# A hybrid decoder layer on one core: the bias row's table loaded by GpSimd, its product moved to the start, the fourth tile turned half a block earlier

## The chip, the cores and the metric

The kernel runs on one core of a Trainium2 chip. Its time is the device time of one execution in microseconds (us); 3 executions of the kernel before gave a median of 664.41 us (664.1 to 664.52). Five engines of the core work side by side, each on its own list of instructions, and wait for each other only through semaphores: TensorE (PE: matrix products, and transposes as products with an identity), ScalarE (ACT), VectorE (DVE), GpSimd (POOL) and SyncE (SP), which here only issues DMAs. GpSimd and ScalarE can issue DMAs too, each into a queue of its own. "Turning" a tile means transposing it on PE.

## The reference

One layer, cut to what matters here. The input is 512 rows of 1024 numbers.

```python
h = rmsnorm(x, norm_pre_mix)                 # (512, 1024)
proj = h @ w_in                              # f, q, i, g; aq, ak, av; indexer iq, ik, iw
y_a = hgrn2_mixer(...)                       # gated linear recurrence, 4 heads of 128
y_b = dsa_mixer(..., rel_bias)               # 128 keys of the indexer's choice per query, 8 heads of 64
    # bias = rel_bias[t5_bucket(qpos - key)] # rel_bias: (32 buckets, 8 heads), added to the logits
x = x + rmsnorm(concat(y_a, y_b) @ w_o, norm_post_mix)
h = rmsnorm(x, norm_pre_ffn)
x = x + rmsnorm((silu(h @ w_gate) * (h @ w_up)) @ w_down, norm_post_ffn)
```

The bias depends only on the distance between query and key. So it is enough to have, for each head, one row of 640 values by distance: the table (32 x 8) turned and multiplied with a one-hot matrix (32 x 640) that says which bucket each distance falls in.

## The kernel before, in words

All float32 numbers are split into a high part (rounded to the format of PE's faster passes) and a low part (the remainder); each large product is then three products: high x low, low x high, high x high. The high part is made on ScalarE by a copy, the low part on VectorE by a subtraction.

**The start.** The 512 rows are four tiles of 128 rows. Each tile t is loaded (`s_x[t]`), squared and summed on ScalarE (`square_in(t)`, L739 and L741), its inverse root is taken on GpSimd (`inv_of`, L617), VectorE scales it with root and gain (`scale_in(t)`, L1096, `s_hx`), PE turns it with eight transposes (`turn_in(t)`, L1670, `s_hps`), ScalarE copies the high part out of PSUM (`turn_hi`, L730, `s_hhi`) and VectorE takes the low part (`turn_lo`, L1089, `s_hlo`). The gain row is spread over the partitions by two products (L1770) ahead of that. Between them PE runs transposes of the identity into an unused bank as fillers (`keep_busy`, L1759).

The first weight chunk (256 columns, `iq`) is loaded and split in two halves of four blocks (`s_raw_half`, `s_raw[0]`; L1101, L631, L745, L1106). PE multiplies it first with the two tiles that are ready (`first_rows(half, m, w, x)`, L1779, 256 columns, four products a call) and later, once the low part of the fourth tile is there (`s_hlo` = 4), with the other two in `feature_group` (L1626). From then on each chunk is done in full by `project(g)` (L1626), 512 columns at a time. Weight chunks come in through a ring of two buffers that SyncE fills (L573), each when the low part of an earlier one is made.

**The bias row.** SyncE loads table and one-hot (L564, L565) behind the tiles and the first chunk, counted on `s_small` together with two other small loads (L562, L563). PE forms the row in two products (L1805, L1806: 8 x 512 and 8 x 128) into banks 6 and 7, ScalarE copies it to SBUF (L758, L759, `s_gsb`), stores it to memory (L763, `s_grow`), and GpSimd later spreads it from there (L652).

Nothing decides the order at run time: each engine's list is in the order in which its program is written, and each DMA queue takes its transfers in order of issue.

Of the kernel before, what the change touches and what calls it, by code (L numbers as in the profile page):

```python
# [7 lines left out]
P = 128  # L8
# [4 lines left out]
ACT = mybir.ActivationFunctionType  # L13

HEADS_A, DK = 4, 128
HEADS_B, DH = 8, 64
# [18 lines left out]
def hymba_layer(nc, x, w_in, lb_logits, hgrn_gnorm, rel_bias, w_o, norm_pre_mix, norm_post_mix,  # L35
                norm_pre_ffn, norm_post_ffn, w_gate, w_up, w_down, onehot, out):
    _, S, D = x.shape
# [69 lines left out]
    with ExitStack() as ctx:  # L107
        def sb(name, shape, dt=F32):
            return ctx.enter_context(nc.sbuf_tensor(name, shape, dt))

        def sem(name):
            return ctx.enter_context(nc.semaphore(name))

        PS = ctx.enter_context(nc.psum_tensor("PS", [P, 8, 512], F32))
# [3 lines left out]
        hT_hi = sb("hT_hi", [P, KT, S], F32R)  # L118
# [81 lines left out]
        oh_sb, tab, g_sb = A2[0:N_BUCKETS, 4096:4736], A2[0:N_BUCKETS, 4736:4744], A2[0:HEADS_B, 4768:5408]  # L200
# [21 lines left out]
        s_ones = sem("row_of_ones")  # L222
        s_gps0 = sem("gain_in_psum")
        s_small = sem("small_landed")
        s_raw = [sem(f"raw_landed{i}") for i in range(2)]
        s_ikw = sem("ikw_raw_landed")
        s_raw_half = sem("first_w_half_landed")
# [23 lines left out]
        s_gps = sem("bias_row_psum")  # L251
        s_gsb = sem("bias_row_sbuf")
# [156 lines left out]
        def ring_of(j):  # L409
            return j if j < J_IKW else j - 1  # L410

        def raw_view(j):
            if j == J_IKW:
                return raw_ikw.rearrange("p (k n) -> p k n", k=KT)
            return view(raw[:, ring_of(j) % 2, :], j)
# [26 lines left out]
        def ring3(n):  # L442
            return W_f[:, RING[n % 3], :]
# [6 lines left out]
        def step_raw(d):  # L450
            return W_f[:, WL[d % 4], :]
# [103 lines left out]
        @block.sync  # L555
        def _(sp):
            for t in range(TB):
                if t == 2:
                    sp.dma_start(raw_view(0)[:, 0:4, :], raw_src(0)[:, 0:4, :]).then_inc(s_raw_half, 16)
                sp.dma_start(xin[:, t, :], x_d[t * P:(t + 1) * P, :]).then_inc(s_x[t], 16)  # L560
            sp.dma_start(raw_view(0)[:, 4:8, :], raw_src(0)[:, 4:8, :]).then_inc(s_raw[0], 16)
            sp.dma_start(lbt[:, :, :], lb_logits.rearrange("r (h p) -> p r h", p=P)).then_inc(s_small, 16)  # L562
            sp.dma_start(gn[:, :], hgrn_gnorm.rearrange("a p -> p a")).then_inc(s_small, 16)  # L563
            sp.dma_start(tab, rel_bias).then_inc(s_small, 16)  # L564
            sp.dma_start(oh_sb, onehot).then_inc(s_small, 16)  # L565
            sp.dma_start(far[:, :], rel_bias[N_BUCKETS - 1, :].partition_broadcast(P)).then_inc(s_far, 16)
            for j in range(1, J_FF + 4):
                if j == J_IKW:
                    sp.dma_start(raw_view(j), raw_src(j)).then_inc(s_ikw, 16)
                    continue  # L570
                if ring_of(j) >= 2:
                    sp.wait_ge(s_lo, j - 2 if j - 2 <= J_IKW else j - 1)
                sp.dma_start(raw_view(j), raw_src(j)).then_inc(s_raw[ring_of(j) % 2], 16)  # L573
            for n, j in enumerate(range(J_FF + 4, J_DN)):
                if n < 2:
                    sp.wait_ge(s_lo, j - 1)
                elif n == 2:
                    sp.wait_ge(s_gu, 8)
                else:
                    sp.wait_ge(s_gu2, 2 * (n - 2))  # L580
                sp.dma_start(view(ring3(n), j), raw_src(j)).then_inc(s_raw3[n % 3], 16)
            for d, (kind, c) in enumerate(STEPS):
                if d == 0:
                    sp.wait_ge(s_gu2, 2 * (NS - 2))
                elif d < 3:
                    sp.wait_ge(s_prod, 3 * (NS - 2 + d))
                elif d == 3:
                    sp.wait_ge(s_gu2, 2 * NS)
                else:
                    steps_done(sp, d - 3)  # L590
                x, y = [wd[(2 * c + k) * P:(2 * c + k + 1) * P, :] for k in range(2)]
                if kind == "one":
                    sp.dma_start(step_raw(d)[:, 0:D], x).then_inc(s_dw[d % 4], 16)
                    sp.dma_start(step_raw(d)[:, D:D + 512], y[:, 512:D]).then_inc(s_dw[d % 4], 16)
                elif kind == "two":
                    sp.dma_start(step_raw(d)[:, 0:D], y).then_inc(s_dw[d % 4], 16)
                else:
                    sp.dma_start(view(step_raw(d), J_DN + c), raw_src(J_DN + c)).then_inc(s_dw[d % 4], 16)
            for t in range(TB):
                for half in range(2):  # L600
                    c = slice(half * 512, (half + 1) * 512)
                    sp.wait_ge(s_fin, 2 * t + half + 1)
                    sp.dma_start(out_d[t * P:(t + 1) * P, c], x2[:, t, c]).then_inc(s_out, 16)
            sp.wait_ge(s_out, 16 * 2 * TB)
# [3 lines left out]
        def _(pool):  # L608
            n_chain = [0]

            def link(ins):
                n_chain[0] += 1
                ins.then_inc(s_pool, 1)
                pool.wait_ge(s_pool, n_chain[0])
# [4 lines left out]
            def inv_root(col, n, width):  # L619
# [3 lines left out]
            link(pool.memset(ident[:, :], 0.0))  # L623
            pool.affine_select(out=ident[:, :], in_=ident[:, :], compare_op=ALU.not_equal, fill=1.0, base=0,
                               pattern=[[-1, P]], channel_multiplier=1).then_inc(s_const, 1)
            link(pool.memset(mhalf[:, :], -0.5))
            for t in range(2):
                pool.wait_ge(s_ss, norm("in", t))
# [93 lines left out]
        def _(act):  # L722
# [5 lines left out]
            def turn_hi(n, banks, t):  # L728
                act.wait_ge(s_hps, n + 1)
                act.activation(hT_hi[:, :, t * P:(t + 1) * P],  # L730
                               PS[:, banks:banks + 2, :].rearrange("p a (k t) -> p (a k) t", t=P),
                               ACT.Copy).then_inc(s_hhi, 1)

            act.dma_start(gain_row, norm_pre_mix).then_inc(s_gin, 16)
            def square_in(t):
                act.wait_ge(s_x[t], 16)
                if t:
                    act.wait_ge(s_sq, t)
                act.activation(ya[:, 0:D], xin[:, t, :], ACT.Square, accum_out=ss[:, t:t + 1]).then_inc(s_sq, 1)  # L739
                act.wait_ge(s_sq, t + 1)  # L740
                act.activation(ms[:, t:t + 1], ss[:, t:t + 1], ACT.Copy, scale=1.0 / D, bias=EPS).then_inc(s_ss, 1)  # L741
# [4 lines left out]

            square_in(0)
            square_in(1)
            turn_hi(0, TURN_BANK[0], 0)
            turn_hi(1, TURN_BANK[1], 1)  # L750
            square_in(2)
# [2 lines left out]
            turn_hi(2, TURN_BANK[2], 2)  # L754
            turn_hi(3, TURN_BANK[3], 3)
            split(1)
            act.wait_ge(s_gps, 1)
            act.activation(g_sb[:, 0:S], PS[0:HEADS_B, 6, :], ACT.Copy)  # L758
            act.activation(g_sb[:, S:S + P], PS[0:HEADS_B, 7, 0:P], ACT.Copy).then_inc(s_gsb, 1)  # L759
            act.wait_ge(s_lbm, 1)  # L760
            act.activation(lbw[:, 1:3, :], lbt[:, :, :], ACT.Exp).then_inc(s_lbe, 1)
            act.wait_ge(s_gsb, 1)
# [311 lines left out]
        def _(dve):  # L1074
# [46 lines left out]
            split_first_rest_lo()  # L1121
            turn_lo(2, TURN_BANK[2], 2)
            turn_lo(3, TURN_BANK[3], 3)
            dve.wait_ge(s_small, 64)
            link(dve.tensor_tensor(lbw[:, 0, :], lbt[:, 0, :], lbt[:, 1, :], ALU.max))
            for r in range(2):
                o = dve.tensor_tensor(lbt[:, r, :], lbt[:, r, :], lbw[:, 0, :], ALU.subtract)
# [495 lines left out]
        def _(pe):  # L1623
# [133 lines left out]
            def keep_busy(bank, n):  # L1757
                for _ in range(n):
                    pe.transpose(PS[:, bank, 0:P], ident[:, :], ident[:, :])  # L1759

            def turn_in(t):
                pe.wait_ge(s_hx, t + 1)
                turn(xin[:, t, :], TURN_BANK[t])
# [5 lines left out]
            for half in range(2):  # L1769
                o = pe.matmul(PS[:, 2 + half, :], pick_last, gain_in_last[:, half * 512:(half + 1) * 512], start=True, stop=True)  # L1770
            o.then_inc(s_gps0, 1)
            keep_busy(1, 9)
            turn_in(0)
            turn_in(1)
            keep_busy(1, 8)

            def first_rows(half, m, w, x):
                for k in range(4 * half, 4 * half + 4):
                    pe.matmul(PS[:, m, 0:S // 2], w[:, k, m * P:(m + 1) * P], x[:, k, 0:S // 2],  # L1779
                              start=(half == 0 and x is hT_hi and w is first_hi and k == 0),  # L1780
                              stop=(half == 1 and x is hT_lo and k == KT - 1))

            first_hi, first_lo = w_split(0)
# [9 lines left out]
                first_rows(0, m, first_hi, hT_lo)  # L1793
            turn_in(2)
            pe.wait_ge(s_hi, 1)
            for m in range(2):
                first_rows(1, m, first_hi, hT_hi)
            turn_in(3)
            pe.wait_ge(s_lo, 1)
            for m in range(2):  # L1800
                first_rows(1, m, first_lo, hT_hi)
            for m in range(2):
                first_rows(1, m, first_hi, hT_lo)
            pe.wait_ge(s_small, 64)
            pe.matmul(PS[0:HEADS_B, 6, :], tab, oh_sb[:, 0:S], start=True, stop=True)  # L1805
            pe.matmul(PS[0:HEADS_B, 7, 0:P], tab, oh_sb[:, S:S + P], start=True, stop=True).then_inc(s_gps, 1)  # L1806
            pe.wait_ge(s_hlo, TB)
            for m in range(2):
                feature_group(w_split(0), m, P, m, S // 2, S, s_proj)
# [291 lines left out]
```

## Time and profile before

| | us |
|---|---|
| median of 3 executions | 664.41 |
| the profiled execution | 664.47 |
| its span | 662.7 |
| PE busy | 652.5 (98% of the span) |
| VectorE busy | 535.2 (81%) |
| ScalarE busy | 343.6 (52%) |
| GpSimd busy | 91.8 (14%) |

The span is the time from the first to the last recorded instruction; 1.77 us of the execution lie around it. The profile is of one execution. In lists of instructions the first number is the start in us from the beginning of the span, the second the duration (several equal instructions that follow each other stand in one row, with xcount), and in brackets stands how long the engine was idle before and what released it. A float32 product is recorded as two pieces, so the two products of L1770 show as x4.

### The profile page before, as it was taken

The page shows a single profiled execution, that of the slowest core. Times are in us where ns is not written, and L with a number is a line of the kernel's source. Part 1 is how long each engine was busy: PE and PEld are TensorE (multiplying, and loading weights), DVE is VectorE, ACT ScalarE, POOL GpSimd, SP SyncE. Part 2 cuts the span into 40 slices and gives each one's busy share as a digit, 9 for nine tenths or more (in the row PEclk, how much of TensorE's full clock was granted, in tenths as well). Part 3 has the DMA queues.
Part 4 walks back from the last instruction along what each step waited for, and adds up shares of the span by engine and source line. Part 5 has one row for each costly group of instructions (what it writes and reads, how often), then busy time and mean ns, then how long its engine had stood idle before and what let it go on. Part 6 is the DMA issues. An engine that isn't in the chain of part 4 may idle for free.

```text
span 662.7 us, 10171 instructions
## 1 busy us (share of the span) xinstructions
PE 652.5 (98%) x4029; PEld 582.1 (88%) x4029; DVE 535.2 (81%) x746; ACT 343.6 (52%) x547; POOL 91.8 (14%) x131
## 2 busy tenths in 40 slices
PE   8999999999999999999999999999999999999996
PEld 6878888888888889888998999999999998888885
DVE  5766999998988768345986988989989879987845
ACT  5656433443349578234653555554555565644532
POOL 4800230000405378002100000000000000000000
PEclk9999999999999999999999999999999999999999
DMA  8443042343521300262342323334234235444513
GB/s 277 129 159 100 29 128 65 96 158 96 190 65 64 121 7 19 110 191 64 98 157 63 105 87 128 93 101 128 77 115 128 68 108 207 158 148 153 164 45 127
DMA packets 50946, 75.01 MB, mean 113 GB/s; under 512 B 5329, under 2 KB 40145, under 8 KB 50642
## 3 DMA queue, kind: packets, MB, share of 16 engines
q1 hardware_dynamic: 47040, 62.26, 29.6%
q0 software_dynamic: 3568, 11.55, 4.7%
q8 instruction: 32, 0.52, 0.3%
q10 hardware_dynamic: 290, 0.55, 0.2%
q14 instruction: 16, 0.13, 0.1%
HBM read 69.60 MB, written 6.84 MB: 115 GB/s over the span
## 4 chain that ended last, share of the span: by engine, by line
PE 94%; DVE 2%; ACT 1%; issue 1%; DMA 1%; POOL 0%; DVEq 0%; POOLq 0%; SPq 0%; ACTq 0%
PE PS L1626 38%; PE PS L1966 27%; PE PS L2004 12%; PE PS L2015 4%; PE PS L1845 2%; PE PS L1700 2%; PE PS L1676 1%; PE PS L1675 1%; PE PS L1856 1%; PE PS L1779 1%; PE PS L1670 1%; DMA A<-in_x_dram 1%; PE PS L1741 1%; PE PS L1710 1%; ACT A L905 1%
## 5 line engine op out<-in xcount | busy, mean ns | idle before, releaser
L1626 PE MATMUL PS<-hT_lo,w_hi 128*128 128x512 f32 (+2 forms) x280 | 102.0, 364 | 0.0
L1626 PE MATMUL PS<-hT_hi,w_hi 128*128 128x512 f32 (+2 forms) x280 | 100.7, 360 | 0.0
L1626 PE MATMUL PS<-hT_hi,w_lo 128*128 128x512 f32 (+2 forms) x280 | 100.7, 359 | 0.0
L1085 DVE TENSOR_TENSOR w_lo<-raw,w_hi 128x2048 fp32r<-128x2048 f32 x21 | 48.1, 2291 | 19.0 <-ACT w_hi L726 18.8
L1966 PE MATMUL PS<-hT_hi,W_r 128*128 128x256 f32 x216 | 61.1, 283 | 0.0
L1966 PE MATMUL PS<-hT_hi,s_w 128*128 128x256 f32 x216 | 61.1, 283 | 0.0
L1966 PE MATMUL PS<-hT_lo,s_w 128*128 128x256 f32 x216 | 61.1, 283 | 0.0
L1626 PEld LDWEIGHTS PS<-hT_hi,w_hi 128*128 128x128 f32 (+1 forms) x280 | 52.5, 188 | 8.4
L1626 PEld LDWEIGHTS PS<-hT_lo,w_hi 128*128 128x128 f32 (+1 forms) x280 | 52.6, 188 | 7.3 <-issue 0.2
L1626 PEld LDWEIGHTS PS<-hT_hi,w_lo 128*128 128x128 f32 (+1 forms) x280 | 52.6, 188 | 7.2
L1966 PE MATMUL PS<-s_t,s_w 128*128 128x256 f32 x288 | 57.8, 283 | 0.6 <-ACT PS L954 0.6
L1966 PEld LDWEIGHTS PS<-s_t,s_w 128*128 128x128 f32 x288 | 47.5, 192 | 0.8 <-issue 0.8
L726 ACT ACTIVATE w_hi<-raw 128x2048 fp32r<-128x2048 f32 x21 | 40.1, 1911 | 14.8 <-PE PS L1626 14.1
L1456 DVE TENSOR_TENSOR W_r<-W_f,s_w 128x1024 fp32r<-128x1024 f32 x36 | 44.0, 1223 | 1.2 <-ACT s_w L939 0.2
L1626 PE MATMUL PS<-w_lo,hT_hi 128*128 128x512 f32 x112 | 44.6, 398 | 0.0
L954 ACT ACTIVATE PS<-PS 128x256 f32<-128x256 f32 x54 | 19.9, 368 | 47.2 <-PE PS L1966 45.6
L1626 PE MATMUL PS<-w_hi,hT_hi 128*128 128x512 f32 x112 | 43.7, 390 | 0.0
L1626 PE MATMUL PS<-w_hi,hT_lo 128*128 128x512 f32 x112 | 43.6, 390 | 0.0
L1966 PEld LDWEIGHTS PS<-hT_lo,s_w 128*128 128x128 f32 x216 | 41.5, 192 | 0.0
L1966 PEld LDWEIGHTS PS<-hT_hi,W_r 128*128 128x128 f32 x216 | 41.5, 192 | 0.0
L1966 PEld LDWEIGHTS PS<-hT_hi,s_w 128*128 128x128 f32 x216 | 41.5, 192 | 0.0
L1966 PE MATMUL PS<-s_t,W_r 128*128 128x256 f32 x144 | 40.7, 283 | 0.0
(306 smaller groups left out, 1685.9 us busy)
## 6 DMA issues: line engine op xcount, KB each, us to landing
raw<-in_w_in_dram SPq DMA_DIRECT2D x15, 1024.0 KB, 5.5
W_f<-in_w_gate_dram SPq DMA_DIRECT2D x9, 1024.0 KB, 5.3
W_f<-in_w_up_dram SPq DMA_DIRECT2D x9, 1024.0 KB, 5.3
W_f<-in_w_down_dram SPq DMA_DIRECT2D x16, 512.0 KB, 3.5
raw<-in_w_o_dram SPq DMA_DIRECT2D x4, 1024.0 KB, 4.9
W_f<-in_w_down_dram SPq DMA_DIRECT2D x3, 1024.0 KB, 4.9
A<-in_x_dram SPq DMA_DIRECT2D x4, 512.0 KB, 6.0
A<-in_x_dram POOLq DMA_DIRECT2D x4, 512.0 KB, 5.6
```

Source lines behind the costliest of these rows:

```text
L726: act.activation(w_split(j)[0], raw_view(j), ACT.Copy).then_inc(s_hi, 1)
L905: act.activation(out, src, ACT.Square, accum_out=ss[:, col:col + 1]).then_inc(s_sqm, 1)
L954: act.activation(to, of, ACT.Copy, scale=scale).then_inc(s_seed, 1)
L1085: dve.tensor_tensor(lo, raw_view(j), hi.bitcast(F32), ALU.subtract).then_inc(s_lo, 1)
L1456: dve.tensor_tensor(block_lo(n)[:, :, c], block_raw(n)[:, :, c], block_hi(n)[:, :, c].bitcast(F32), ALU.subtract).then_inc(s_wl[2 if i els ...
L1626: o = pe.matmul(out, lhs[a], rhs[b], start=(first and n == 0), stop=(last and n == 2))
L1670: o = pe.transpose(PS[:, bank + k // 4, (k % 4) * P:(k % 4 + 1) * P], src[:, k * P:(k + 1) * P], ident[:, :])
L1700: o = pe.matmul(PS[:, level_bank(l, p), h * P:(h + 1) * P], a, late(l)[:, m * P:(m + 1) * P], start=True, stop=True)
L1845: o = pe.matmul(PS[:, 4 + b % 2, h * DH:(h + 1) * DH], PT[u % 2][:, s * P:(s + 1) * P], av[:, s * W + h * DH:s * W + (h + 1) * DH], start= ...
L1966: o = pe.matmul(out, (hi, lo)[a][:, k, :], xs[b][:, k, :], start=(fresh and k == 0 and p == 0), stop=(k == 3 and p == 2), skip_group_check ...
L2004: o = pe.matmul(PS[:, bank + 2 * t, :], (hi, lo)[a][:, t * P:(t + 1) * P], w[b], start=(start and p == 0), stop=(p == 2), skip_group_check ...
L2015: o = pe.matmul(PS[:, 2 * t + half, :], x[a][:, k, t * P:(t + 1) * P], w[b][:, k, half * 512:(half + 1) * 512], start=False, stop=(p == 2) ...
```

## The change

Four edits, all in the first 22 us of the program.

1. Table and one-hot are loaded by GpSimd, right after it has made the identity, on a semaphore of their own (`s_tab`). SyncE no longer loads them; VectorE waits for two small loads on `s_small` where it waited for four.
2. PE forms the bias row right behind the gain row's products, ahead of the first tile's turning, into banks 0 and 1. The 9 fillers there become 4, in bank 7. The row's two products behind the first rows are gone. PE waits for the copied row (`s_gsb`) ahead of the 8 fillers that follow the second tile's turning.
3. ScalarE copies the row to SBUF behind the squares of the first two tiles. Its store stays where it was.
4. The fourth tile is turned between the two high x high groups of the second half, where it was turned behind both.

```diff
@@ SyncE
             sp.dma_start(gn[:, :], hgrn_gnorm.rearrange("a p -> p a")).then_inc(s_small, 16)
-            sp.dma_start(tab, rel_bias).then_inc(s_small, 16)
-            sp.dma_start(oh_sb, onehot).then_inc(s_small, 16)
@@ GpSimd
                                pattern=[[-1, P]], channel_multiplier=1).then_inc(s_const, 1)
+            pool.dma_start(tab, rel_bias).then_inc(s_tab, 16)
+            pool.dma_start(oh_sb, onehot).then_inc(s_tab, 16)
             link(pool.memset(mhalf[:, :], -0.5))
@@ ScalarE
             square_in(1)
+            act.wait_ge(s_gps, 1)
+            act.activation(g_sb[:, 0:S], PS[0:HEADS_B, 0, :], ACT.Copy)
+            act.activation(g_sb[:, S:S + P], PS[0:HEADS_B, 1, 0:P], ACT.Copy).then_inc(s_gsb, 1)
             turn_hi(0, TURN_BANK[0], 0)
...
             split(1)
-            act.wait_ge(s_gps, 1)
-            act.activation(g_sb[:, 0:S], PS[0:HEADS_B, 6, :], ACT.Copy)
-            act.activation(g_sb[:, S:S + P], PS[0:HEADS_B, 7, 0:P], ACT.Copy).then_inc(s_gsb, 1)
@@ VectorE
-            dve.wait_ge(s_small, 64)
+            dve.wait_ge(s_small, 32)
@@ TensorE
             o.then_inc(s_gps0, 1)
-            keep_busy(1, 9)
+            pe.wait_ge(s_tab, 32)
+            pe.matmul(PS[0:HEADS_B, 0, :], tab, oh_sb[:, 0:S], start=True, stop=True)
+            pe.matmul(PS[0:HEADS_B, 1, 0:P], tab, oh_sb[:, S:S + P], start=True, stop=True).then_inc(s_gps, 1)
+            keep_busy(7, 4)
             turn_in(0)
             turn_in(1)
+            pe.wait_ge(s_gsb, 1)
             keep_busy(1, 8)
...
             pe.wait_ge(s_hi, 1)
-            for m in range(2):
-                first_rows(1, m, first_hi, hT_hi)
+            first_rows(1, 0, first_hi, hT_hi)
             turn_in(3)
+            first_rows(1, 1, first_hi, hT_hi)
             pe.wait_ge(s_lo, 1)
...
-            pe.wait_ge(s_small, 64)
-            pe.matmul(PS[0:HEADS_B, 6, :], tab, oh_sb[:, 0:S], start=True, stop=True)
-            pe.matmul(PS[0:HEADS_B, 7, 0:P], tab, oh_sb[:, S:S + P], start=True, stop=True).then_inc(s_gps, 1)
             pe.wait_ge(s_hlo, TB)
```

What this does to the order on PE behind the gain row's products, before (PS is PSUM; A holds tiles, table and one-hot; h_ready is `s_hx`):

```order
L1770 MATMUL PS<-A 128x512
L1759 MATMUL PS<-ident 128x128 x9
L1670 MATMUL PS<-ident,A 128x128 [waits h_ready]
L1670 MATMUL PS<-ident,A 128x128 x7
L1670 MATMUL PS<-ident,A 128x128 [waits h_ready]
```

and in the changed kernel, whose line numbers stand one to five higher:

```order
L1771 MATMUL PS<-A 128x512
L1774 MATMUL PS<-A 8x512 [waits bias_table_landed]
L1775 MATMUL PS<-A 8x128
L1760 MATMUL PS<-ident 128x128 x4
L1671 MATMUL PS<-ident,A 128x128 [waits h_ready]
L1671 MATMUL PS<-ident,A 128x128 x7
L1671 MATMUL PS<-ident,A 128x128 [waits h_ready]
```

The two bias products stand behind a wait for the table, and both turnings stand behind them.

The second place on PE, from the third tile's turning to the first full group, before:

```order
L1670 MATMUL PS<-ident,A 128x128 x7
L1779 MATMUL PS<-hT_hi,w_hi 128x256 [waits w_hi_ready]
L1779 MATMUL PS<-hT_hi,w_hi 128x256 x7
L1670 MATMUL PS<-ident,A 128x128 [waits h_ready]
L1670 MATMUL PS<-ident,A 128x128 x7
L1779 MATMUL PS<-hT_hi,w_lo 128x256 [waits w_lo_ready]
L1779 MATMUL PS<-hT_hi,w_lo 128x256 x7
L1779 MATMUL PS<-hT_lo,w_hi 128x256 x8
L1805 MATMUL PS<-A 8x512 [waits small_landed]
L1806 MATMUL PS<-A 8x128
L1626 MATMUL PS<-hT_lo,w_hi 128x256 [waits hT_lo_ready]
```

and in the changed kernel:

```order
L1671 MATMUL PS<-ident,A 128x128 x7
L1784 MATMUL PS<-hT_hi,w_hi 128x256 [waits w_hi_ready]
L1784 MATMUL PS<-hT_hi,w_hi 128x256 x3
L1671 MATMUL PS<-ident,A 128x128 [waits h_ready]
L1671 MATMUL PS<-ident,A 128x128 x7
L1784 MATMUL PS<-hT_hi,w_hi 128x256 x4
L1784 MATMUL PS<-hT_hi,w_lo 128x256 [waits w_lo_ready]
L1784 MATMUL PS<-hT_hi,w_lo 128x256 x7
L1784 MATMUL PS<-hT_lo,w_hi 128x256 x8
L1627 MATMUL PS<-hT_lo,w_hi 128x256 [waits hT_lo_ready]
```

The fourth tile's eight transposes stand four products sooner, and the full group follows the first rows directly.

On GpSimd, in the changed kernel, the two loads stand between the identity and the first root, for which it waits on ScalarE:

```order
L623 AFFINE_SELECT ident<-ident 128x128
L625 DMA A<-in_rel_bias_dram 32x8
L626 DMA A<-onehot_dram 32x640
L627 MEMSET mhalf 128x16
L616 TENSOR_TENSOR rstd<-ms,mhalf 128x1 [waits sumsq_ready,pool_chain]
```

Before, the identity, the small constant and the root followed each other with no DMA between.

## Rows read from the trace of the kernel before

**Rows 1.** The page, busy time of each engine, share of the span, instructions.
```profile
PE 652.5 (98%) x4029; PEld 582.1 (88%) x4029; DVE 535.2 (81%) x746; ACT 343.6 (52%) x547; POOL 91.8 (14%) x131
```
**Rows 2.** Waits of PE after 22 us: who <- whom: us, times, longest.
```profile
PE PS L1966 <- ACT PS L954: 0.6, 1, 0.6
...
PE PS L1845 <- DVE A L383: 0.2, 1, 0.2
```
**Rows 3.** Chain that ended last, 0 to 60 us: start, us, what.
```profile
1.23 5.02 DMA A<-in_x_dram
...
6.27 1.16 ACT A L739 x2
...
8.32 1.29 DVE A L1096
...
11.96 3.11 PE PS L1779 x24
```
**Rows 4.** Timeline of PE, 0 to 24 us: start, us, instruction, idle before.
```profile
2.49 3.70 PE L1770 MATMUL PS<-A 97*128 97x512 f32 x4
5.99 1.33 PE L1759 MATMUL PS<-ident 128*128 128x128 f32 x9
8.21 1.09 PE L1670 MATMUL PS<-ident,A 128*128 128x128 f32 x8 [0.89 <-DVE A L1096]
9.65 1.10 PE L1670 MATMUL PS<-ident,A 128*128 128x128 f32 x8 [0.36 <-DVE A L1096]
...
16.97 1.04 PE L1670 MATMUL PS<-ident,A 128*128 128x128 f32 x8
...
18.80 1.12 PE L1779 MATMUL PS<-hT_lo,w_hi 128*128 128x256 f32 x8
19.84 1.02 PE L1805 MATMUL PS<-A 32*8 32x512 f32 x2
...
21.01 0.38 PE L1626 MATMUL PS<-hT_lo,w_hi 128*128 128x256 f32 x1
```
**Rows 5.** Timeline of ScalarE, 0 to 24 us.
```profile
7.45 0.20 ACT L741 ACTIVATE ms<-ss 128x1 f32<-128x1 f32 x1
...
9.33 1.03 ACT L730 ACTIVATE hT_hi<-PS 128x1024 fp32r<-128x1024 f32 x1 [1.68 <-PE PS L1670]
...
18.04 1.03 ACT L730 ACTIVATE hT_hi<-PS 128x1024 fp32r<-128x1024 f32 x1 [0.80 <-PE PS L1670]
18.96 1.90 ACT L726 ACTIVATE w_hi<-raw 128x2048 fp32r<-128x2048 f32 x1
21.12 0.59 ACT L758 ACTIVATE A<-PS 8x512 f32<-8x512 f32 x1 [0.25 <-PE PS L1806]
21.61 0.25 ACT L759 ACTIVATE A<-PS 8x128 f32<-8x128 f32 x1
```
**Rows 6.** Timeline of VectorE, 0 to 24 us.
```profile
13.74 2.56 DVE L1096 SCALAR_TENSOR_TENSOR A<-A,rstd,PS 128x1024 f32<-128x1024 f32 x2 [0.68 <-POOL rstd L617]
...
19.10 1.23 DVE L1089 TENSOR_TENSOR hT_lo<-PS,hT_hi 128x1024 fp32r<-128x1024 f32 x1 [0.53 <-ACT hT_hi L730]
```
**Rows 7.** Timeline of GpSimd, 0 to 24 us.
```profile
1.24 0.29 POOL L624 TENSOR_SCALAR_AFFINE_SELECT ident<-ident 128x128 f32<-128x128 f32 x1 [0.24 <-POOL ident L623]
```
**Rows 8.** Line L673, GpSimd's eight 128 KB loads: issue ns, then landing.
```profile
L673 POOL DMA_DIRECT2D A<-bias_by_distance x8: 549/559/584, 168.7 to 172.4; - x8
...
DMA to landing us min/median/max: 2.3/2.4/5.5
```
**Rows 9.** DMA queue (packets, MB, share) and issues (size, us to landing).
```profile
q0 software_dynamic: 3568, 11.55, 4.7%
...
A<-onehot_dram SPq DMA_DIRECT2D x1, 80.0 KB, 4.3
...
lbt<-in_lb_logits_dram SPq DMA_DIRECT2D x1, 4.0 KB, 8.0
```
**Rows 10.** Stretch 4 to 5 us: PE, PEld, DVE, ACT, POOL busy, clock, DMA share, GB/s.
```profile
4.00:5.00 1.00, 1.00 (x2) 0.34 (x1) 0.00 (x0) 0.35 (x1) 0.00 (x0) 1.00 0.97 379
```

More of the change, by code:

```diff
@@ L224, in hymba_layer @@
         s_small = sem("small_landed")
+        s_tab = sem("bias_table_landed")
         s_raw = [sem(f"raw_landed{i}") for i in range(2)]
```

## The prediction, made before the changed kernel was run

> **What bounds the kernel now.** I read the page first: TensorE (PE) is busy 98% of the span [rows 1], so a change pays only where it takes PE time away or lets PE's work start sooner. The list of PE's waits after 22 us names three in all, of 0.6 us at the most and 0.2 at the least [rows 2]: from the first projection on, PE is never short of anything for longer. Whatever brings the first full projection group (L1626) forward brings the end forward by the same amount, and whatever delays it delays the end. So the case is decided in the first 21 us, and there I read the chain [rows 3]. The reader is to see two kinds of stretch. Up to 11.96 us the chain is latency: the second input tile lands at 6.25 (1.23 + 5.02), ScalarE squares it, GpSimd makes its root, VectorE scales it by 9.61, PE turns it, ScalarE copies it. From 11.96 on it is PE without a gap, and its last pieces before L1626 are the bias row's two products, L1805 and L1806.
>
> **Part 1: the bias row leaves the packed stretch.** On PE the last first-rows group starts at 18.80; its eight products run at (19.84 - 18.80) / 8 = 0.13 us each. Then L1805 starts at 19.84, L1806 follows, and L1626 starts at 21.01 [rows 4]. Taken out, this frees 21.01 - 19.84 = 1.17 us on the path.
>
> **Part 2: what is late next.** L1626 needs the low part of the fourth tile (h_lo 4), which VectorE finishes at 19.10 + 1.23 = 20.33 [rows 6]. With part 1 alone PE would stand from 19.84 to 20.33 and only 21.01 - 20.33 = 0.68 of the 1.17 us would be won. The change moves the fourth tile's turning ahead of four products, 4 x 0.13 = 0.52 us: from 16.97 to 16.45. Its input is there, since the two scalings end at 13.74 + 2.56 = 16.30 [rows 6]. ScalarE starts 1.07 us after the turning starts (18.04 - 16.97), so at 17.52; it was idle for 0.80 us before 18.04, so free from 17.24 [rows 5]. VectorE starts 1.06 us after ScalarE, at 18.58; it was idle for 0.53 us before 19.10, so free from 18.57. It ends at 19.81. PE is ready at 19.84. Three engines fit with 0.01 to 0.3 us to spare, so I charge 0.05 us for a handover that doesn't quite fit: the gain of parts 1 and 2 is 1.12 us, between 0.68 (the sooner turning helps nothing) and 1.17. Work on PE between the two turnings is reordered, not added.
>
> **Part 3: the bias row in its new place.** PE has now 1.17 us for the two products and 4 fillers at 1.33 / 9 = 0.15, 0.59 us, between 5.99 and the first tile's turning at 8.21; it had 9 fillers, 1.33 us, and a wait of 0.89 us [rows 4]. 5.99 + 1.17 + 0.59 = 7.75, before 8.21. That costs nothing, if the table is there. The deadline: the second tile's turning starts at 9.65 and the first takes 1.09 before it, so the fillers may end at 8.56, the products may start at 8.56 - 1.76 = 6.80. ScalarE's copies (0.59 + 0.25, [rows 5]) lie between the end of its small operation, 7.45 + 0.20 = 7.65, and 9.33: 1.68 us of room for 0.84. The new wait for the copied row ahead of the 8 fillers asks, at 9.65 + 1.10 = 10.75, for something that is done well before; behind it fillers and the first rows are queued, and nobody else waits for them sooner than before.
>
> When does the table land? GpSimd is free at 1.24 + 0.29 = 1.53 [rows 7] and has nothing to do until ScalarE has squared the first tile, so two issues cost it nothing. An issue takes 0.55 us [rows 8], so the one-hot's starts at 2.08. From issue to landing, GpSimd's eight 128 KB loads took 2.3 us at the least: 4.4. The slowest of them took 5.5: 7.6 [rows 8]. The one-hot itself took 4.3 us from SyncE's queue: 6.4 [rows 9]. I take 5.5 us on the clock of the span, between the first and the last of these: no wait. At the upper end the wait would cost 7.6 - 6.8 = 0.8 us.
>
> **Part 4: what the early load does to the second tile.** This is the cost I expect. From 4 to 5 us the DMA engines are 0.97 busy at 379 GB/s [rows 10], and they are carrying the second tile, on which the chain hangs. The loads' 81 KB are now in that traffic: 81 x 1024 / 379000 = 0.22 us, if they go through ahead of the tile's last packets. Below stands 0 (they fill gaps, or land behind the tile). Above: a packet of GpSimd's queue takes 4.7% x 16 x 662.7 / 3568 = 0.14 us on the mean [rows 9]; 64 rows over 16 engines are 4 packets each, 0.56 us. I take 0.22. The cast, the low half on GpSimd and the third tile all hang on the same chain and move with it. The later loads have slack.
>
> Row for row this case shows only one small transfer in another queue than SyncE's at this time: the gain row from ScalarE's queue, whose product on PE starts at 2.49, while the 4 KB lbt load in SyncE's queue took 8.0 us behind the tiles [rows 4, 9]. The Trainium skill (DMA: Bandwidth & Descriptors, section on queues, rings and completion order) has each engine serve its queues in turn, a packet at a time; by it the table need not wait for what SyncE has asked for, and takes its share from the tile, as parts 3 and 4 have it. Without the rule's turn-taking, the table would come behind the tiles: the second rival. The two rows agree with the rule but don't prove it, since the gain row left before the traffic was full.
>
> **Part 5: the rest, at nothing.** SyncE's queue loses two issues, so the second weight chunk is asked for sooner; ScalarE takes it up at 18.96 right behind the fourth tile's copy, with no wait [rows 5], so it was there anyway. VectorE's wait counts two loads instead of four, asked for first. The store of the bias row stays where it was, and so does its reader.
>
> **Sum.** -1.12 + 0.22 = -0.90 us. The profiled execution took 664.47 (span 662.7 and 1.77 around it), 0.06 above the median 664.41 of the runs. So 664.41 - 0.90 = **663.5 us**, 0.14% less.
>
> **The rivals.**
> - *Full gain.* The table's packets don't touch the second tile, and the handover fits: -1.17, 663.2. For it: 80 KB is little beside the 2 MB asked for. Against: the queue is full at 4 to 5 us.
> - *The table lands late, and PE waits for it (slower side).* One mechanism: the transfer is served only after what SyncE asked for earlier, as lbt was. The price: lbt took 8.0 us [rows 9]; 2.08 + 8.0 = 10.1. Then products and fillers to 11.9, the first turning to 13.0, and the second starts at 13.0 in place of 9.65: +3.3 - 1.12 = +2.2, 666.6. It decides from 6.80 on, eats the gain at 7.9, and is slower by over 0.2% (1.33 us) from 9.25 on. A landing at 7.6 gives +0.8 - 1.12 = -0.3, 664.1. Against: the 4.3 and 2.3 us above.
> - *The clock.* The four pieces of the gain product take (5.99 - 2.49) / 4 = 0.88 us each from start to start; the two of L1805, as wide, take 1.02 us together [rows 4]. That is about half speed before 5.99, the 1.2 GHz level, though the granted clock reads 1.00 from 4 to 5 us too [rows 10]. If with 4 fillers instead of 9 and a wait for the table the clock drops back or comes later, the 24 products from 11.96 on (3.11 us) take twice as long: +3.1 - 0.9 = +2.2, 666.6. The Trainium skill (TensorE: Matmul & The Clock Gate, section on what is actually happening) has activity release the clock and idleness take it back. Against: PE is busy 1.76 us there in place of 1.33, if the table is in time.
> - *The fourth tile isn't turned to effect* (any of its three engines is late by the 0.5 us): -0.68 + 0.22, 663.9. It stays inside the forecast's own range.
>
> **How the numbers follow.** Forecast (with the last rival, 663.2 to 664.1) 0.60. Full gain or a little over it, 0.18. Table in part late, near 664.1: 0.11. Table behind the tiles 0.06, clock 0.05. What a measurement of this kernel can tell from no change is about 0.2%, 1.33 us: 663.1 and 665.7. My arithmetic allows 1.17 us, so faster by over 0.2% needs a little more than I can find or a small difference between measurements: 0.15. Slower by over 0.2% needs one of the last two: 0.09. Within it: 0.76. The range 662.9 to 665.0 leaves out the two slow rivals and a little below.
>
> **What would show it.** In the changed profile: (1) the gain product ends near 6.0 and the bias products start with no gap over 0.8 us; (2) ScalarE's square of the second tile starts at 6.4 to 6.5 instead of 6.27 [rows 3], and everything to the first products (11.96) is late by the same; (3) the fourth tile's turning starts about 0.5 us sooner against the third's; (4) the distance from the first products to L1626 falls from 21.01 - 11.96 = 9.05 to about 7.93; (5) PE's waits behind 22 us stay near 1.1 us. I am wrong if the square starts after 6.9, if the turnings wait for the table, or if L1626 starts on time and the end is not sooner.

## The result, and the profile after

The changed kernel took 666.93 us (median of 6 executions, 666.18 to 667.65), against 664.38 for the kernel before beside it: a ratio of 1.0038 with a 95% interval of 1.0028 to 1.0048. It is 2.55 us slower. A second measurement on another occasion gave 666.70 against 664.40, ratio 1.0032 (1.0020 to 1.0045). The forecast was 0.9 us faster. The profiled execution took 666.32 us, its span is 664.6 (662.7 before). Of g1 and g4 below, one execution each took 1079.94 and 919.56 us at a mean granted clock of 0.56 and 0.66; the ratios leave these out, the medians given don't, and without them they would be 663.40 and 663.74.

The chain that ended last, of the changed kernel, 0 to 24 us (start, us, what), answers to [rows 3]:

```profile
1.75 0.69 POOL A L625
2.44 5.05 DMA A<-onehot_dram
7.49 0.04 issue
7.53 1.87 PE PS L1774 x2
9.40 0.43 PE PS L1775 x2
9.83 1.04 PE PS L1760 x4
10.87 2.97 PE PS L1671 x16
13.84 0.02 issue
13.86 1.03 ACT hT_hi L731
14.89 0.14 issue
15.03 3.11 PE PS L1784 x24
```

The chain begins with another piece: not the second input tile but the one-hot matrix, on which PE waits until 7.49. Then everything up to 13.86 hangs on PE, where it hung on VectorE and ScalarE before. PE's timeline of the changed kernel in the same stretch answers to [rows 4]:

```profile
3.25 3.75 PE L1771 MATMUL PS<-A 97*128 97x512 f32 x4 [0.55 <-DMA A<-in_norm_pre_mix_dram]
7.53 1.87 PE L1774 MATMUL PS<-A 32*8 32x512 f32 x2 [0.53 <-DMA A<-onehot_dram]
9.20 0.63 PE L1775 MATMUL PS<-A 32*8 32x128 f32 x2
9.76 1.11 PE L1760 MATMUL PS<-ident 128*128 128x128 f32 x4
10.66 3.16 PE L1671 MATMUL PS<-ident,A 128*128 128x128 f32 x16
...
15.03 1.19 PE L1784 MATMUL PS<-hT_hi,w_hi 128*128 128x256 f32 x8 [0.33 <-ACT hT_hi L731]
...
21.87 1.12 PE L1784 MATMUL PS<-hT_lo,w_hi 128*128 128x256 f32 x8
22.98 0.39 PE L1627 MATMUL PS<-hT_lo,w_hi 128*128 128x256 f32 x1
```

Two things are to be seen. The row's first product takes 1.87 us where it took 1.02, and fillers and turnings are slow too: PE runs at half rate here. And from 15.03 on all is as forecast: the first full group starts 22.98 - 15.03 = 7.95 us behind the first products, where it was 21.01 - 11.96 = 9.05.

How many PE instructions start in a microsecond shows where the rate comes back; PE's stretches of 1 us of the changed kernel (busy, instructions, granted clock, DMA share, GB/s):

```profile
11.00:12.00 1.00, 1.00 (x7) 1.00 1.27 217
12.00:13.00 1.00, 1.00 (x6) 1.00 1.12 210
13.00:14.00 1.00, 1.00 (x11) 1.00 1.05 343
```

Six or seven of the same small instructions up to 13 us, eleven in the next microsecond: the step to double rate lies shortly behind 13.0. In the kernel before it lay near 6.3, inside the nine fillers, which take 1.33 us there and 1.15 in f2 and g1 below, where the step came sooner. The clock column reads 1.00 on both sides of the step, so durations have to be read here, not that column. The reason is that the trace's first record of the clock, at full, begins only with the step: at 13.2 us in the changed kernel, at 6.3 in the kernel before.

So the loss is in place: the first products are 15.03 - 11.96 = 3.07 us late, of which 9.05 - 7.95 = 1.10 is won back. That leaves 1.97; the span grew by 1.9. PE's waits behind 24 us are the three of [rows 2], unchanged.

A second profile of the changed kernel (h3 below, 667.31 us) tells the same with larger numbers: PE waits 1.31 us for the one-hot and starts the row at 8.34, the step comes at 14.4, and the first full group starts at 23.98.

### The profile page after: what moved, and what is told of

It reads as the page before. It is cut to its first block, busy times and chain, and to the rows that moved or that the text cites. A ratio compares the mean times of both kernels' runs of the same rounds, so it can differ in the third digit from the quotient of the medians.

```text
span 664.6 us, 10161 instructions
## 1 busy us (share of the span) xinstructions
PE 654.5 (98%) x4024; PEld 583.1 (88%) x4024; DVE 535.1 (81%) x746; ACT 343.4 (52%) x547; POOL 93.1 (14%) x133
## 4 chain that ended last, share of the span: by engine, by line
PE 94%; DVE 2%; issue 1%; ACT 1%; DMA 1%; POOL 0%; DVEq 0%; POOLq 0%; ACTq 0%
PE PS L1627 38%; PE PS L1968 27%; PE PS L2006 12%; PE PS L2017 4%; PE PS L1847 2%; PE PS L1701 2%; PE PS L1677 1%; PE PS L1676 1%; PE PS L1858 1%; PE PS L1671 1%; PE PS L1784 1%; DMA A<-onehot_dram 1%; PE PS L1742 1%; PE PS L1711 1%; ACT A L906 1%
```

## The experiments

Two causes were suspected: the table lands late, and PE stays at half rate. A third was that GpSimd's loads hold up the gain row. Half rate is the lower level of PE's clock, 1.2 GHz; the bias row's products are called thin, since they use 32 rows and 8 columns where a filler uses 128 and 128. All kernels were timed beside the kernel before; a median is followed by that of the kernel before on the same occasion.

**f1: the sooner turning alone.**

```diff
-            for m in range(2):
-                first_rows(1, m, first_hi, hT_hi)
+            first_rows(1, 0, first_hi, hT_hi)
             turn_in(3)
+            first_rows(1, 1, first_hi, hT_hi)
```

> The kernel before with one edit alone: the fourth tile is turned between the two high x high groups of the second half. The bias row's products stay behind the first rows. Every theory of the loss (late table, slow clock, late gain row) lies in the other edits, so all expect the time of before, 664.4, within 0.2 us: the low part of the fourth tile is ready about 0.5 us sooner, but PE is still busy with the bias row until 21.0 us. If this run is slower by over 0.5 us, part of the loss is in the reordering and all three are incomplete.

Measured 664.18 (664.27), ratio 1.0002 (0.9993 to 1.0011): no difference. In its profile the gain product starts at 3.18 us, though this kernel has no early loads:

```profile
3.18 3.75 PE L1770 MATMUL PS<-A 97*128 97x512 f32 x4 [0.48 <-DMA A<-in_norm_pre_mix_dram]
```

The gain row's landing thus varies by itself between executions: its product starts at 2.5 or 3.2 us. The edit is harmless. But this profile shows what a late gain row goes with. The list on PE up to the first rows is that of the kernel before, nine fillers and no product of the bias row among them, and still PE is at half rate for most of it:

```profile
6.72 2.13 PE L1759 MATMUL PS<-ident 128*128 128x128 f32 x9
8.64 2.53 PE L1670 MATMUL PS<-ident,A 128*128 128x128 f32 x16
```

The step comes at 9.9 us, and the first full group starts at 21.47 in place of 21.01. This execution took 664.94 us, one of three near 665; the other seven lie between 663.99 and 664.23.

**f2: the early loads alone**, the products in their old place.

```diff
-            sp.dma_start(tab, rel_bias).then_inc(s_small, 16)
-            sp.dma_start(oh_sb, onehot).then_inc(s_small, 16)
...
+            pool.dma_start(tab, rel_bias).then_inc(s_tab, 16)
+            pool.dma_start(oh_sb, onehot).then_inc(s_tab, 16)
```

> The kernel before with the loads alone moved: GpSimd loads table and one-hot at the start; the products stay where they were, behind the first rows. Theory 'late table' (PE's wait is the loss): nobody waits for the table here, 664.4 within 0.3. Theory 'clock' (gap and thin products at the start keep PE at half rate): neither is there, 664.4 within 0.3, and PE at full rate from about 6 us. Theory 'gain row' (GpSimd's loads hold up the 4 KB gain row, so that its product starts at 3.2 instead of 2.5 us and the clock comes late): the product starts at 3.2, fillers and turnings of the first two tiles run at half rate, and the time is 1 to 2 us above before, 665.4 to 666.4.

Measured 664.31 (664.27), ratio 1.0002 (0.9993 to 1.0011), the gain product at 2.48: no cost of the loads is seen (the interval would let up to 0.7 us pass), and the theory that they hold up the gain row, with 1 to 2 us of loss, falls. But its one-hot took longer still to land, 7.3 us from an issue at 2.4, so 9.7 (issue, size, us to landing):

```profile
A<-onehot_dram POOLq DMA_DIRECT2D x1, 80.0 KB, 7.3
A<-in_rel_bias_dram POOLq DMA_DIRECT2D x1, 1.0 KB, 5.3
```

**f3: the changed kernel without the wait for the table.** The bias row is zero.

```diff
-            pe.wait_ge(s_tab, 32)
-            pe.matmul(PS[0:HEADS_B, 0, :], tab, oh_sb[:, 0:S], start=True, stop=True)
+            pe.matmul(PS[0:HEADS_B, 0, :], pick_last[0:32, 0:8], gain_in_last[0:32, 0:S], start=True, stop=True)
...
```

> The changed kernel with the two bias products fed from zeros of the same shape that are in SBUF already, so that they need not wait for the table; the bias row is zero. The loads are issued as in the changed kernel and waited for at the first full group. Theory 'late table': the wait was the loss; products start when the gain product ends, turnings on time, 663.3 (1.1 below before). Theory 'clock' in the form that the gap ahead of the products keeps the rate down: no gap, full rate from about 6, 663.3 too. Theory 'clock' in the form that products with 32 rows and 8 columns don't count as work: half rate until past 9 us although there is no gap; the row's products and fillers take 3 us in place of 1.8 and the turnings twice their time: 665 to 666. Theory 'gain row': product at 3.2, all at half rate: 665 to 666, with the gain product late.

Measured 665.55 (664.27), ratio 1.0021 (1.0011 to 1.0031). The wait is gone and more than a microsecond of loss stays, so the late table is not all of it. PE's timeline of f3:

```profile
2.49 3.70 PE L1771 MATMUL PS<-A 97*128 97x512 f32 x4
6.12 1.87 PE L1773 MATMUL PS<-A 32*8 32x512 f32 x2
7.79 0.63 PE L1774 MATMUL PS<-A 32*8 32x128 f32 x2
8.35 1.11 PE L1760 MATMUL PS<-ident 128*128 128x128 f32 x4
9.26 2.91 PE L1671 MATMUL PS<-ident,A 128*128 128x128 f32 x16
```

There is no gap on PE from 1.58 to 12 us, the gain product starts at 2.49 as in the kernel before, and yet the product takes 1.87 us and the fillers 1.11. So a gap isn't needed for the late step. Whether the gaps of the changed kernel add to it, f3 doesn't tell.

**f4: nine more fillers ahead of the wait** (`keep_busy(7, 9)` in front of it).

> The changed kernel with nine more fillers ahead of the wait for the table, so that PE works while it waits. Theory 'late table': if the gain product ends at 6.0 the fillers end at 7.3, the table is there at 7.5, and the row costs 0.7 of the 1.1 us won: 664.0. Theory 'clock' (the gap): full rate comes back to about 6 us, 664.0, against 666.9 for the changed kernel. Theory 'clock' (thin products): as the gap theory unless the rate falls again behind the fillers. Theory 'gain row': the gain product ends at 7.0 at half rate, nine fillers at 0.24 us end at 9.1, and all comes later still: 667.5 to 668.5.

Measured 665.73 (664.27), ratio 1.0024 (1.0011 to 1.0038). None of the numbers fits well. Its profile has the product at full rate (1.02 us) at 8.23, and the first full group at 20.99, as in the kernel before; but also a wait of 1.1 us of PE for VectorE late in the kernel (at L2007), which the other profiles don't have or have with 0.2. I count it as showing that the rate is mended in the profiled execution, and not for the size of the wait; i1 below was made for that. What makes its median so high stays open.

**g1: both causes taken away**: products as in f3, nine fillers ahead, none behind.

```diff
-            pe.wait_ge(s_tab, 32)
+            keep_busy(7, 9)
...
-            keep_busy(7, 4)
```

> The changed kernel without the wait for the table (products fed from zeros, bias row zero, as in f3) and with the 9 fillers of before ahead of the row's products, none behind. Both suspected causes are gone: nothing waits for the load, and ahead of the turnings PE runs full-size products. Theory 'two causes' (late table and low rate behind thin products, each costing some 1.3 us and not adding up fully): full rate from 6 to 8 us, fillers end near 7.3, products at 8.5, turnings on time, first full group near 19.9: 663.2 to 663.6. Theory 'a third cause' (anything else in the new order at the start, such as bank use or the copy on ScalarE): still above 664.5.

Measured 663.52 (664.15), ratio 0.9995 (0.9983 to 1.0007). The median is in the forecast of two causes (663.2 to 663.6), the interval of the ratio doesn't tell the kernel from the one before. First full group at 19.73. A third cause in the row's new place, of the size of the loss, is not there.

**g2: f3 with products that fill the array.**

```diff
-            pe.matmul(PS[0:HEADS_B, 0, :], pick_last[0:32, 0:8], gain_in_last[0:32, 0:S], start=True, stop=True)
+            pe.matmul(PS[:, 0, :], pick_last, gain_in_last[:, 0:S], start=True, stop=True)
...
```

> As f3 (no wait for the table, products right behind the gain product, 4 fillers), but with stand-in products that fill the array like the gain product's: 97 rows and 128 columns of stationary instead of 32 and 8, same number of moving columns. The bias row holds the gain row's numbers. Theory 'thin products hold the clock down': these count as full work, the rate rises where it rises in the kernel before, the turnings are on time and the gain of 1.1 us shows: 663.2 to 663.6, against 665.55 for f3. Theory 'too few fillers, whatever the products are' (or: the rise comes at its own moment): as f3, 665 to 666, half rate until about 11 us.

Measured 663.30 (664.15), ratio 0.9988 (0.9979 to 0.9998). This is the sharpest pair: same order, same moving columns, same 4 fillers, no wait in either. PE's timeline of g2:

```profile
2.49 3.70 PE L1771 MATMUL PS<-A 97*128 97x512 f32 x4
5.98 1.44 PE L1773 MATMUL PS<-A 97*128 97x512 f32 x2
7.26 0.38 PE L1774 MATMUL PS<-A 97*128 97x128 f32 x2
7.48 0.60 PE L1760 MATMUL PS<-ident 128*128 128x128 f32 x4
```

Behind products of 97 rows by 128 columns PE is at full rate before 7.3 us; behind products of 32 by 8 it is at half rate until about 11. The difference in time is 665.55 - 663.30 = 2.25 us, over two occasions whose kernels before differ by 0.12. No execution of f3 (664.73 and more) was as fast as the slowest of g2 (664.64).

**g3: table and one-hot through ScalarE's queue**, behind the gain row.

> The changed kernel with the table and the one-hot loaded from ScalarE's queue, right behind the gain row, instead of by GpSimd. Theory 'late table alone': the load lands by 5 or 6 us, PE doesn't wait: 663.3. Theory 'two causes': the wait goes, the thin products at low rate stay, as in f3: 665.0 to 665.8. If the load delays the first input tile or ScalarE's first square, the square starts later than 4.5 us and the time rises by as much.

Measured 666.73 (664.15), ratio 1.0030 (1.0020 to 1.0041). Neither forecast fits, since the wait did not go. Another queue doesn't help: issued at 1.75, the one-hot took 5.4 us and landed at 7.15. And here the records show the clock itself. PE's timeline of g3, then its stretches of 1 us:

```profile
7.23 1.02 PE L1774 MATMUL PS<-A 32*8 32x512 f32 x2 [1.26 <-DMA A<-onehot_dram]
8.09 0.38 PE L1775 MATMUL PS<-A 32*8 32x128 f32 x2
8.40 0.66 PE L1760 MATMUL PS<-ident 128*128 128x128 f32 x4
8.90 3.49 PE L1671 MATMUL PS<-ident,A 128*128 128x128 f32 x16
```

```profile
6.00:7.00 1.00, 0.00 (x0) 1.00 1.19 343
7.00:8.00 1.00, 0.77 (x2) 1.00 0.99 388
8.00:9.00 1.00, 1.00 (x8) 1.00 1.00 401
9.00:10.00 1.00, 1.00 (x7) 0.51 1.04 382
10.00:11.00 1.00, 1.00 (x7) 0.50 1.13 303
11.00:12.00 1.00, 1.00 (x7) 0.50 1.31 157
12.00:13.00 1.00, 1.00 (x9) 0.78 1.07 334
```

The rate had come (the product takes 1.02 us), PE stood 1.26 us for the table, ran the thin products, and at 9 us the granted clock fell to 0.50, the 1.2 GHz level, until past 12. So the same order can lose the clock after having had it. This is the fastest of g3's eight executions (665.15); what the others did isn't on record.

**g4: another place for the row.** The kernel before's head with 9 fillers; the row's 384 columns that are read later in bank 1 in place of fillers behind the second turning; VectorE copies them; the first rows go one column block after the other.

```diff
-            pe.wait_ge(s_gsb, 1)
-            keep_busy(1, 8)
+            keep_busy(1, 3)
+            pe.wait_ge(s_tab, 32)
+            pe.matmul(PS[0:HEADS_B, 1, 0:NEAR + P], tab, oh_sb[:, S - NEAR:S + P], start=True, stop=True).then_inc(s_gps, 1)
+            keep_busy(0, 2)
...
```

> A version that avoids both suspected causes: the head of the kernel before (9 fillers), GpSimd's early loads, and the bias row formed in place of fillers behind the second tile's turning, at 10.7 us, when the table has landed even at its slowest (9.7) and PE is at full rate. Only the 384 columns that are read later are formed, in bank 1; VectorE copies them behind the second tile's low part, and the first rows go column block by column block so that bank 1 is free for so long. The fourth tile is turned sooner. Theory 'two causes': gain of 1.1 us less up to 0.3 for the first rows' new order: 663.3 to 663.6 against 664.3. Theory 'a third cause' (the row's early place itself costs): above 664.3.

Measured 663.82 (664.15), ratio 0.9991 (0.9981 to 1.0001): at or a little below the kernel before, the interval just reaches no change.

**h1: both causes mended in the real kernel.** SyncE loads table and one-hot behind the first two tiles; 9 fillers ahead of the wait, none behind. **h2** is the same with 384 columns. **h3** is the changed kernel again.

```diff
                 if t == 2:
+                    sp.dma_start(tab, rel_bias).then_inc(s_tab, 16)
+                    sp.dma_start(oh_sb, onehot).then_inc(s_tab, 16)
...
```

> The changed kernel with both causes mended and the computation whole: SyncE loads table and one-hot right behind the first two input tiles (issue at 1.7 and 2.1 us, ahead of the first weight half), and PE runs the 9 fillers of before ahead of the wait for the table, none behind the products. Theory 'two causes' (landing after 6.8 us costs, thin products at low rate cost): the table lands between 6 and 7, fillers end at about 7.0, products at about 8.2, turnings on time, first full group near 19.8: 663.3 to 663.8, about as g1. If the load still lands at 8 or later in this place of SyncE's queue, PE waits and the time is 664.5 to 665.7, as in f4; then only the rate is mended.

> As h1, with only the 384 columns of the bias row that are read later: one product of 8 x 384 in place of 8 x 512 and 8 x 128, one copy on ScalarE, a load of 48 KB in place of 80. Theory 'two causes': the row is done some 0.5 us sooner than in h1, so it has room even when the table lands at 7.3: 663.1 to 663.6, at or below h1. If it is no better than h1, the wait for the table was hidden in h1 already.

> The changed kernel as it is, beside h1 and h2 on one chip, for a direct comparison. All theories: 666.5 to 667.2, over 2 us above before; the table lands between 7 and 9 us, and PE is at half rate for some of the time between 7 and 13 us.

Measured beside 664.40: h1 663.77, ratio 0.9995 (0.9984 to 1.0006); h2 664.15, ratio 1.0004 (0.9993 to 1.0015); h3 666.70. In h1 the one-hot landed at 2.16 + 4.4 = 6.6 us and PE doesn't wait for it. Its executions lie apart, from 663.01 to 667.42, where those of the kernel before lie between 664.14 and 665.19. h2 is no better than h1, which says the wait was hidden in h1 already. Both are level with the kernel before within what could be measured. In h1's profile (664.48) the forecast place of the first full group, 19.8, was missed too: it starts at 21.20. The table was there, but the gain row landed late, its product starts at 3.47, and the step comes at 8.6; h2's profile has 3.32 and 8.1.

**i1: g1 with the real table and its wait.**

```diff
+            keep_busy(7, 9)
             pe.wait_ge(s_tab, 32)
...
-            keep_busy(7, 4)
```

> g1 with the real table and the wait for it (loads by GpSimd): 9 fillers ahead of the wait, none behind the products. It differs from g1 in the wait alone, so it prices the wait by itself with the rate mended. Landings in these kernels lay between 7.5 and 9.7 us, g1 starts its products at 6.7. Theory 'two causes': products at 8.2 to 8.6, late by 1.5 to 1.9, of which up to 0.5 is room before the first turning: 1.0 to 1.9 us above g1, 664.5 to 665.4, clearly below the changed kernel's 666.8. If it is within 0.3 us of g1, the wait costs nothing once PE works through it. If it is at 666.5 or more, the rate falls again while PE waits, and the fillers mend nothing.

Measured 664.58 (664.20), ratio 1.0015 (1.0004 to 1.0027). PE's wait for the table, of i1:

```profile
PE PS L1775 <- DMA A<-onehot_dram: 0.9, 1, 0.9
```

Seven of its 12 executions lie between 663.83 and 664.66, four between 666.56 and 667.49. Others of these kernels have such executions too: g1 one (666.80), h1 one, h2 three above 666. They would fit a rate that falls as in g3 or returns late; none of them has a profile, so that is not shown.

Put together, as distances of each median from that of the kernel before on the same occasion (us):

| | table waited for | not waited for |
|---|---|---|
| thin products, 4 fillers behind | +2.55, +2.30 (changed) | +1.28 (f3) |
| 9 fillers ahead, none behind | +0.38 (i1) | -0.63 (g1) |
| 9 fillers ahead, 4 behind | +1.46 (f4) | |
| products that fill the array | | -0.85 (g2) |

The wait costs 1.0 to 1.3 us in the first two rows, the rate 1.9 to 2.2 between them and 2.1 between f3 and g2. -0.63 + 1.0 + 1.9 = +2.3. The gain of the profile, 1.10, shows only in part in the medians of g1 and g2, and f4 fits in badly: four fillers more than i1, 0.5 us of work, and 1.1 us slower.

**Where the step to full rate lies**, from the first clock record of each trace (the counts of instructions per microsecond agree with it), against the start of the gain product (us):

| profile | gain product | full rate from |
|---|---|---|
| f2, g1 | 2.5 | 5.2 |
| g3 | 2.5 | 5.6 (half again from 9.0 to 12.4) |
| before | 2.5 | 6.3 |
| g2 | 2.5 | 6.8 |
| f4, i1 | 2.5 | 7.4, 7.5 |
| f3 | 2.5 | 11.3 |
| h2, h1 | 3.3, 3.5 | 8.1, 8.6 |
| g4 | 3.2 | 9.2 |
| f1 | 3.2 | 9.9 |
| changed, twice | 3.3 | 13.2, 14.4 |

Two things are to be seen that the pairs above don't show. The kernel before, f2, g1, f4 and i1 give PE the same work up to the end of the nine fillers, and the step still scatters from 5.2 to 7.5. And in all six profiles in which the gain row landed late, so that PE stood 0.5 to 0.8 us ahead of its product, the step lies at 8.1 or later, in f1 and g4 at 9.2 and 9.9 though they have nine fillers and no thin product ahead of it. Both profiles of the changed kernel are among these six. So thin products are shown to cost 2.1 us (f3 against g2, with the gain row in time in both profiles); how much of the changed kernel's late step goes with its late gain row, and how often that row is late, no run shows.

## Why the prediction was wrong

**Parts 1 and 2, the gain: right.** 9.05 - 7.95 = 1.10 us was forecast as 1.12. The handover is as tight as it was said to be. In the medians of g1 and g2, with both costs taken away, 0.63 and 0.85 of it are left. VectorE's low parts of tiles 3 and 4 in the changed kernel:

```profile
20.43 2.49 DVE L1090 TENSOR_TENSOR hT_lo<-PS,hT_hi 128x1024 fp32r<-128x1024 f32 x2
```

They end at 22.92 and the full group starts at 22.98.

**Part 3 failed, in two steps.** The first: "I take 5.5 us on the clock of the span". The one-hot landed at 7.49 in the profiled execution, and between 8.1 and 9.7 in the other kernels that load all of it by GpSimd. Its issue started at 2.44 instead of 2.08: the first issue of the queue took 0.69 us and began 0.23 late. From there it took 5.0 to 7.3 us, where 5.5 on the clock meant 3.4 from the issue, less than either small load of [rows 9] had taken. Those two, 4.3 for the one-hot behind the tiles and 8.0 for lbt among them, give 6.4 and 10.1; every landing lies between. The queue alone doesn't explain lbt: from SyncE's own queue, third in line, the one-hot took 4.4 us (h1). The Trainium skill (DMA: Bandwidth & Descriptors, section on the anatomy of one DMA, GpSimd's path) gives such a load a fixed 2 us and its bytes; an estimate by it is 2.2 us for 80 KB. The trace has 5.0 and more beside the input tiles' loads, so that figure doesn't hold here. Serving queues in turn did not bring the table quickly either: 1 KB took 4.1 us and more.

The second step is worth more: "5.99 + 1.17 + 0.59 = 7.75". The 1.17 us of the two products was read at 20 us, at full rate, and put at 6 to 8 us. There the products took 9.76 - 7.53 = 2.23 us, the fillers 0.90, and the turnings that follow were slow too. The working, from the deadlines of part 3: start 7.53 - 6.80 = 0.73 late, of which the gain product, ended at 7.00, would have cost 0.20 without the table; products and fillers (10.66 - 7.53) - 1.76 = 1.37; what is left of 3.07, 0.97, is the turnings at half rate.

**The clock rival was the right mechanism at a wrong place.** It had a chance of 0.05 and its time was 666.6, near the 666.93 measured. That the number is so near is luck. I priced it at the 24 products behind 11.96, which run at full rate (3.11 us before and after), and argued against it with PE's busy time. f3 is busy without a gap and still slow; g2 differs only in how much of the array the products use, and is fast. The slow stretch was ahead of those products, in the row's own products, the fillers and the turnings. The Trainium skill (TensorE: Matmul & The Clock Gate, section on what is actually happening) has activity release the clock and idleness take it back; the trace agrees where g3 falls to 0.50 behind a wait, but in f3 PE stood nowhere and was at half rate until about 11 us.

**Part 4, the second tile: no cost seen.** Its square starts at 5.78 in the changed kernel and at 5.70 to 6.50 in the other profiles with GpSimd's early loads; without them it starts at 5.99 (f1) and 6.27 [rows 3]. What scatters by 0.8 us by itself shows nothing of the 0.22 us forecast, and f2's interval is too wide to tell it from nothing. Which of the two it is stays open; it isn't the loss.

**The late-table rival** was right that the load comes late, at 1.0 to 1.3 us rather than the 3.3 given; the landing is at 7.5 to 9.7, not 10.1.

**The range** of 662.9 to 665.0 left both out because each was taken for unlikely by itself. Here both came in one kernel, and their costs add.

## What to carry to other kernels

A duration of PE holds for the rate at which it was read. Before moving a product to the start of a kernel, compare the same instruction at both places, and look in the profile for where the rate returns and which work stands ahead of that. In this kernel products of 32 x 8 did not stand in for fillers. A small load asked for among the input tiles took 3.4 to 7.3 us here, in whichever of three queues it went: what PE needs at 6 us has to be asked for that much earlier, or ahead of the tiles. And one profile is one execution: the step to full rate lay up to 2.3 us apart in profiles with the same work ahead of it.

## What the runs showed of the hardware that was not expected

- With the same number of moving columns, PE was at half rate until about 11 us behind products with a 32 x 8 stationary (f3, 1.87 us for the 512-column product) and at full rate before 7.3 us behind 97 x 128 (g2, 1.44 us, the step falls inside it): 2.25 us of kernel time between the medians.
- With the same work on PE ahead of it, the step to full rate lay at 5.2, 5.2, 6.3, 7.4 and 7.5 us (f2, g1, before, f4, i1). In the six profiles in which PE had stood 0.5 to 0.8 us for the gain row, it lay between 8.1 and 14.4.
- The granted clock reads 1.00 in stretches in which instructions take twice as long, where no change of the clock is on record yet; of the stretches ahead of the first full group, only those of g3, which had risen and fell again, show 0.50.
- A 1 KB load took 4.1 to 5.4 us and an 80 KB load 5.0 to 7.3 us from GpSimd's queue at the start; ScalarE's queue took 4.2 and 5.4, SyncE's, third in line, 4.2 and 4.4. The gain row's product starts at 2.5 us in some executions and 3.2 to 3.5 in others, with the same instructions ahead of it.
- A kernel can be less steady than its median tells: the kernel before kept to 0.4 us in its first six executions, to 1.8 us beside f1 to f4 and to 1.1 us beside i1; i1 spread over 3.7.
